# Attention: strided groups laid out residue by residue, rotary sums on GpSimd, exponentials written to PSUM; HGRN gates kept in PSUM

## The reference, cut to what matters

```python
# HGRN2 gates (layer 0)
forget = lb + (1.0 - lb) * sigmoid(f)
key = 1.0 - forget
log_f = log(forget)
query = silu(q)

# dilated attention (layer 1): 12 heads in 3 groups of 4; DILATED_GROUPS = ((128, 1), (512, 4), (2048, 16))
q = apply_rope(qkv[:, :, 0], cos, sin)          # x1*cos - x2*sin, x2*cos + x1*sin
k = apply_rope(qkv[:, :, 1], cos, sin)
# per group: tokens are taken by residue class mod dilation; banded, causal window on each
scores = where(mask, q @ k.T * 128 ** -0.5, -inf)
m = max(scores); p = exp(scores - m); l = sum(p)
out = (p @ v) / l;  lse = m + log(l)
# the three groups' outputs are weighed by softmax(lse) over the groups
o = (stack(outs) * softmax(lse)).reshape(B, S, ATTN_WIDTH) @ w_out
```

## Time and profile before

| | |
|---|---|
| median of 3 runs | 2152.67 us (2152.38 to 2156.83) |
| profiled execution | 2158.04 us |
| its span | 2156.2 us |
| PE busy | 2120.2 us (98%) |
| DVE busy | 995.1 us (46%) |
| ACT busy | 868.8 us (40%) |
| POOL busy | 1149.7 us (53%) |

### The profile page before, as it was taken

How to read it: one execution, slowest core, us unless ns; L and a number is a source line. 1 busy time by engine, 2 the same in 40 slices (tenths; PEclk the granted TensorE clock), 3 DMA queues, 4 the chain that set the end, 5 groups by cost and what they waited for, 6 DMA issues and landing times. The chain is left out here.

```text
span 2156.2 us, 28081 instructions
## 1 busy us (share of the span) xinstructions
PE 2120.2 (98%) x10271; PEld 1750.4 (81%) x10271; DVE 995.1 (46%) x1562; ACT 868.8 (40%) x1250; POOL 1149.7 (53%) x642
## 2 busy tenths in 40 slices
PE   7999999999999999999999999999999999999998
PEld 6788878888888988888888888888667888888886
DVE  6666564403442057745422436563783344422433
ACT  7677653312233234434322334453764234322323
POOL 5677755545554465455554565473224555554552
PEclk9999999999999999999999999999999999999999
DMA  6122133322332322133332332322102223332332
GB/s 214 59 68 68 59 97 94 107 93 88 97 108 80 96 88 69 57 105 98 97 106 89 98 106 89 120 72 89 69 21 79 97 89 98 97 108 85 94 112 70
DMA packets 54423, 195.65 MB, mean 91 GB/s; under 512 B 6832, under 2 KB 9664, under 8 KB 53952
## 3 DMA queue, kind: packets, MB, share of 16 engines
q1 hardware_dynamic: 52864, 187.27, 27.7%
q10 hardware_dynamic: 1472, 7.19, 0.9%
HBM read 190.25 MB, written 4.19 MB: 90 GB/s over the span
## 5 line engine op out<-in xcount | busy, mean ns | idle before, releaser
L1764 POOL TENSOR_TENSOR w_split<-ring,w_split 128x1024 fp32r<-128x1024 f32 (+3 forms) x327 | 841.3, 2573 | 827.1 <-ACT w_split L1237 827.0
L1237 ACT CAST w_split<-ring 128x1024 fp32r<-128x1024 f32 (+3 forms) x327 | 356.4, 1090 | 1007.6 <-PE ps L498 876.1
L496 PE MATMUL ps<-u_split,w_split 128*128 128x512 f32 x1768 | 705.5, 399 | 10.5 <-DVE u_split L2019 9.8
L498 PE MATMUL ps<-u_split,w_split 128*128 128x512 f32 x1768 | 691.0, 391 | 0.0
L497 PE MATMUL ps<-u_split,w_split 128*128 128x512 f32 x1768 | 690.8, 391 | 0.0
L496 PEld LDWEIGHTS ps<-u_split,w_split 128*128 128x128 f32 x1768 | 333.6, 189 | 87.6 <-issue 16.9
L498 PEld LDWEIGHTS ps<-u_split,w_split 128*128 128x128 f32 x1768 | 333.2, 188 | 70.5
L497 PEld LDWEIGHTS ps<-u_split,w_split 128*128 128x128 f32 x1768 | 333.8, 189 | 69.6 <-issue 3.1
L496 PE MATMUL ps<-hid,w_split 128*128 128x512 f32 x637 | 249.0, 391 | 1.5 <-POOL hid L1959 1.4
L498 PE MATMUL ps<-hid,w_split 128*128 128x512 f32 x637 | 247.9, 389 | 0.0
L497 PE MATMUL ps<-hid,w_split 128*128 128x512 f32 x637 | 247.9, 389 | 0.0
(11 more groups left out here) (355 smaller groups left out, 2511.1 us busy)
## 6 DMA issues: line engine op xcount, KB each, us to landing
ring<-in_w_hgrn SPq DMA_DIRECT2D x32, 512.0 KB, 3.6
ring<-in_w_attn_qk SPq DMA_DIRECT2D x24, 512.0 KB, 3.5
ring<-in_w_merge SPq DMA_DIRECT2D x24, 512.0 KB, 3.3
ring<-in_w_gu0a SPq DMA_DIRECT2D x22, 512.0 KB, 3.6
ring<-in_w_gu0b SPq DMA_DIRECT2D x22, 512.0 KB, 3.5
ring<-in_w_gu1a SPq DMA_DIRECT2D x22, 512.0 KB, 3.6
ring<-in_w_gu1b SPq DMA_DIRECT2D x22, 512.0 KB, 3.5
ring<-in_w_gu2a SPq DMA_DIRECT2D x22, 512.0 KB, 3.5
```

Source lines behind the costliest of these rows:

```text
L496: nc.tensor.matmul(ps[:, bank], ws[:, 0, r, w], act[:, 0, c], start=c == 0, stop=False)
L498: m = nc.tensor.matmul(ps[:, bank], ws[:, 1, r, w], act[:, 0, c], start=False, stop=c == n - 1)
L1237: nc.scalar.copy(ws[:, 0, slot, 0:w], ring[:, r, 0:w]).then_inc(s["w_hi"], 1)
L1764: nc.gpsimd.tensor_tensor(ws[:, 1, slot, 0:w], ring[:, r, 0:w], ws[:, 0, slot, 0:w].bitcast(F32), ALU.subtract).then_inc(s["w_lo"], 1)
```

## The change

- `forget` is written back into the PSUM bank of the sigmoid instead of `fg`; `key` is made from there, and the logarithm works in place in that bank, after `key`. The new branches ask `isinstance(head, int)`. `hgrn_forget` and `hgrn_log` are called with a number for heads 0 and 1 alone, ahead of the loop over heads; the calls for heads 2 to 7 stand in the loop and pass pairs, so these keep the old path.
- All query and key tiles except the key tile of group 0 (N % 6 == 1) are written by residue, so that the score matmuls of groups 1 and 2 read 128 neighbouring columns.
- The sum of the rotary step goes from DVE to POOL, behind the cosine product of the same tile. DVE's sine products wait for the sum of tile N-2, as they overwrite its input.
- The exponentials are written to the score banks in PSUM instead of over the masked scores in SBUF; L2419 and L2425 read them there.
- In ACT's list the cast of tile N+5 goes ahead of the wait for the group maxima (`mix_diff`); in the last round so does the cast of `attn_out` unit 3.

```diff
@@ -807,11 +807,10 @@
                         pe.wait_ge(s["ao_lo"], 3 * (j - 1) + (3, 1, 2)[g])
                     q, k = QK[j % 2][:, 2 * g], QK[j % 2][:, 2 * g + 1]
                     for b in range(TT):
+                        qb = q[:, b * P:(b + 1) * P]
                         if g:
-                            m = nc.tensor.matmul(SC_BANKS[g][:, b], q[:, tokens(g, b)], k[:, tokens(g, b)],
-                                                 start=True, stop=True)
+                            m = nc.tensor.matmul(SC_BANKS[g][:, b], qb, k[:, b * P:(b + 1) * P], start=True, stop=True)
                             continue
-                        qb = q[:, b * P:(b + 1) * P]
                         if b:
                             m = nc.tensor.matmul(SC_BANKS[0][:, b], qb, k[:, (b - 1) * P:(b + 1) * P], start=True, stop=True)
                         else:
@@ -1416,6 +1415,10 @@
                 nc.scalar.activation(dst, src, ACT.Sigmoid).then_inc(s[done], 1)
 
             def hgrn_log(head, dst):
+                if isinstance(head, int):
+                    act.wait_ge(s["key"], cnt(head, 1, 1))
+                    nc.scalar.activation(dst, dst, ACT.Ln).then_inc(s["log_f"], 1)
+                    return
                 act.wait_ge(s["forget"], cnt(head, 1, 1))
                 nc.scalar.activation(dst, fg, ACT.Ln).then_inc(s["log_f"], 1)
 
@@ -1518,7 +1521,7 @@
                 act.wait_ge(s["sc_negmax"], 3 * j + score_order(j).index(g) + 1)
                 for b in range(TT):
                     neg, total = (own0[:, k, b:b + 1] if g == 0 else stats[:, k, g, b:b + 1] for k in range(2))
-                    nc.scalar.activation(SC[g][:, b], SC[g][:, b], ACT.Exp, bias=neg, accum_out=total
+                    nc.scalar.activation(SC_BANKS[g][:, b], SC[g][:, b], ACT.Exp, bias=neg, accum_out=total
                                          ).then_inc(s["p_exp"], 1)
 
             for n in range(6):
@@ -1531,20 +1534,21 @@
                 if more:
                     exps(j, 0)
                     exps(j, 1)
+                    qk_weights(N + 5)
                 else:
                     exps(j, 1)
                     hi("attn_out", 2)
                     exps(j, 0)
                     exps(j, 2)
+                    hi("attn_out", 3)
                 act.wait_ge(s["mix_diff"], j + 1)
                 nc.scalar.activation(e_mix, e_mix, ACT.Exp).then_inc(s["mix_exp"], 1)
                 if more:
-                    qk_weights(N + 5)
                     exps(j, 2)
                     take_raw(N + 3, weights=False)
                     take_raw(N + 4)
                 else:
-                    for k in range(3, 6):
+                    for k in range(4, 6):
                         hi("attn_out", k)
                 for n, g in enumerate((1, 2, 0)):
                     act.wait_ge(s["pt_ps"], 3 * j + n + 1)
@@ -1883,8 +1887,19 @@
                     pool.wait_ge(s["rope_scaled"], 2)
                 nc.gpsimd.tensor_tensor(raw[:, N % 2], raw[:, N % 2], cos_a[:], ALU.mult).then_inc(s["rope_cos"], 1)
 
+            def rotary_sum(N):
+                if N >= 12:
+                    pool.wait_ge(s["sc_ps"], 3 * (N // 6 - 1))
+                pool.wait_ge(s["rope_sin"], 2 * N + 2)
+                pool.wait_ge(s["rope_cos"], N + 1)
+                qk, x, y = QK[N // 6 % 2][:, N % 6], raw[:, N % 2], tsin[:, N % 2]
+                if N % 6 != 1:
+                    qk, x, y = by_query(N % 6 // 2, qk), in_order(x), in_order(y)
+                nc.gpsimd.tensor_tensor(qk, x, y, ALU.add).then_inc(s["qk_ready"], 1)
+
             for n in range(24):
                 times_cos(n)
+                rotary_sum(n)
             for k in range(2, 6):
                 lo("attn_out", k)
 
@@ -2269,9 +2284,10 @@
                 x = (head if isinstance(head, int) else head[1]) % 2
                 col = bass.ds(head[0] * 2 + head[1], 1) if not isinstance(head, int) else slice(head, head + 1)
                 dve.wait_ge(s["sig_f"], cnt(head, 1, 1))
-                nc.vector.tensor_scalar(fg, gate, omlb[:, col], lb[:, col], ALU.mult, ALU.add).then_inc(s["forget"], 1)
+                forget = gate if isinstance(head, int) else fg
+                nc.vector.tensor_scalar(forget, gate, omlb[:, col], lb[:, col], ALU.mult, ALU.add).then_inc(s["forget"], 1)
                 dve.wait_ge(s["forget"], cnt(head, 1, 1))
-                nc.vector.tensor_scalar(key[x], fg, -1.0, 1.0, ALU.mult, ALU.add).then_inc(s["key"], 1)
+                nc.vector.tensor_scalar(key[x], forget, -1.0, 1.0, ALU.mult, ALU.add).then_inc(s["key"], 1)
 
             def hgrn_query(head, gate):
 
@@ -2366,16 +2382,12 @@
 
             def rope(N):
                 dve.wait_ge(s["raw_ready"], N + 1)
+                if N >= 2:
+                    dve.wait_ge(s["qk_ready"], N - 1)
                 for lower in (0, 64):
                     src, dst = slice(lower, lower + 64), slice(64 - lower, 128 - lower)
                     nc.vector.tensor_tensor(tsin[dst, N % 2], ps[src, qk_bank(N)], sin_a[src], ALU.mult
                                             ).then_inc(s["rope_sin"], 1)
-                dve.wait_ge(s["rope_sin"], 2 * N + 2)
-                dve.wait_ge(s["rope_cos"], N + 1)
-                qk, x, y = QK[N // 6 % 2][:, N % 6], raw[:, N % 2], tsin[:, N % 2]
-                if N % 6 == 0:
-                    qk, x, y = by_query(0, qk), in_order(x), in_order(y)
-                nc.vector.tensor_tensor(qk, x, y, ALU.add).then_inc(s["qk_ready"], 1)
 
             def masked_max(j, g):
                 n = score_order(j).index(g)
@@ -2416,13 +2428,13 @@
                 dve.wait_ge(s["mix_steps"], 4 * j + 4)
                 both = scm[:, 1024:2048].rearrange("p (b n) -> p b n", b=2 * TT)
                 w12 = e_mix[:, 1:3].rearrange("p g b -> p (g b)")[:, :, None]
-                nc.vector.tensor_tensor(both, both, w12.broadcast_to((P, 2 * TT, P)), ALU.mult).then_inc(s["p_norm"], 1)
+                nc.vector.tensor_tensor(both, ps[:, 6:8].rearrange("p a (b n) -> p (a b) n", b=TT), w12.broadcast_to((P, 2 * TT, P)), ALU.mult).then_inc(s["p_norm"], 1)
                 for r in range(RESIDUES):
                     for b in range(TT):
                         m = nc.vector.tensor_copy(w0[32 * r:32 * r + 32, b:b + 1], e_mix[32 * b:32 * b + 32, 0, r:r + 1])
                 m.then_inc(s["swapped_back"], 1)
                 dve.wait_ge(s["swapped_back"], j + 1)
-                nc.vector.tensor_tensor(SC[0], SC[0], w0[:, :, None].broadcast_to((P, TT, 2 * P)), ALU.mult
+                nc.vector.tensor_tensor(SC[0], SC_BANKS[0], w0[:, :, None].broadcast_to((P, TT, 2 * P)), ALU.mult
                                         ).then_inc(s["p_norm"], 1)
 
             def ao_rest(j):
```

## The result

| | before | after |
|---|---|---|
| median | 2151.86 us (19 runs, 2148.43 to 2156.83) | 2155.21 us (19 runs, 2153.57 to 2157.14) |
| profiled execution | 2158.04 us | 2154.19 us |
| its span | 2156.2 us | 2152.4 us |

The ratio is 1.0019, with a 95% interval from 1.0013 to 1.0024. So the changed kernel is 3 to 5 us slower, where 9.9 us of gain were forecast, and its median lies 4 us above the range. The two profiled executions compare the other way round (2154.19 against 2158.04). That contrast is the first half of the answer: the profiled execution of before was not like most of its executions.

A forecast was written before the change was run, and what follows sets the result against it. PE, busy 2120.2 of 2156.2 us, was taken as the bound. -7.1 (HGRN) -7.0 (scores) +4.2 (waits) = -9.9 us took the profiled 2158.04 to 2148.1; with the median 5.4 lower, 2142.8, range 2136 to 2151.

The forecast's parts named there:

- The 5.2 us: PE's single wait on the HGRN score gather (L2186), traced to head 1's key product taking 9.11 us on DVE beside POOL.
- change 1: HGRN gates of heads 0 and 1 in PSUM: removes 5.15 us of wait and 1.9 of half clock, together 7.1.
- Rival E: HGRN: PE finds another late releaser at 53 us, gain 0 of 7.1, 2149.9 us; chance 0.08.
- Change 2: Attention score matmuls of groups 1 and 2 read contiguous columns: 1.76 us saved a round, 7.0 in four rounds.
- Change 3: Rotary sums moved from DVE to POOL: 1.4 us each, so POOL's cycle of 5.1 fits PE's tile of 5.44.
- Rivals C and D: Rotary sum on POOL takes about 2.1 us: 2149.8, chance 0.09; or 2.6, pacing all 24 tiles: 2162, chance 0.06.
- The round worked out: Attention round 0 scheduled by hand: PE waits 0.6 for group 0's probabilities and 1.1 for cast 12; all rounds +4.2 us.
- rival B: Attention: POOL also blocks the 16 mix copies, chain ends some 2.6 us later, 7.8 in three rounds, 2150.6; chance 0.15.
- The cast itself: Cast 11 moved ahead in ACT's list: pays for itself, avoiding 1.6 us a round, with no gain beyond the matmul saving.
- rival A: POOL doesn't get in DVE's way at L2401 and L2414 in attention: 5.6 us less, 2137.2; chance 0.20.
- Waits behind the core: PE waits after attention's core for the next cast: 1.1 us in round 0; tile 23's sum 0.5 late in round 3.
- Change 4: Attention exponentials written to PSUM: under 0.1 us a round, counted as nothing; effect is 0.9 and the blocking within the round.

The follow-up runs named there:

- one-element experiment: The changed kernel with each of the 16 two-element copies of the mix split into two one-element copies: 2147.03 us, ratio 0.9983 to before.
- layout alone: The kernel before with only tiles written by residue and contiguous score matmuls of groups 1 and 2, sums still on DVE: 2154.97 us, ratio 1.0019.
- second profile of before: The kernel before, nothing edited, profiled once more: 2152.72 us, span 2150.9.
- copies as reductions: The changed kernel with the 16 two-element copies of the mix done as maxima over one element: 2146.31 us, ratio 0.9964 to before.
- exponentials back in SBUF: The changed kernel with exponentials written over the masked scores in SBUF and read there by the two products: 2158.11 us, ratio 1.0039 to before.
- attention alone: The changed kernel without its HGRN lines, so HGRN as before: 2159.58 us, ratio 1.0028 to before.
- moved cast back: The changed kernel with the cast of tile N+5 back behind the mix exponential in ACT's list: 2150.84 us, ratio 0.9999 to before.
- the version that beats both: copies as reductions, plus POOL's low part of the first unit behind the core put ahead of the sum: 2143.89 us, ratio 0.9968 to before.
- HGRN alone: The kernel before with only the diff's HGRN lines (heads 0 and 1 through PSUM): 2150.3 us, ratio 0.9985.
- sums back on DVE: The changed kernel with the rotary sums back on DVE, still written by residue: 2154.54 us, ratio 1.0004 to before.

## Why the prediction was wrong, point by point

**What bounds it: right.** PE's program, its waits and the clock behind them are the only places where the time changed.

**The 5.2 us, and change 1: the mechanism right, its weight in the median wrong.** `key` from PSUM takes 0.69, the scans follow at 48.1, no wait and no low clock are left near 60. The term of -7.1 was real in the profiled execution and is absent from most. The clue was on the table: the profiled execution took 5.4 us more than the median, and the wait was 5.15. I carried those 5.4 us over as a constant to both kernels, where they were the wait itself. Where the wait is there, 7.1 was the right size (6.7 us between the two profiles of before). The right term for a median is about 1 us. Rival E's price was thus nearly right, but by luck, as its mechanism was not: no other releaser took over, and PE reached that point on time.

**Change 2: right.** 64 matmuls from 15.7 to 7.9 us of duration, and 1.7 us a round in the distance of starts.

**Change 3, the price of the sum: right.** Its 24 instances took (ns, min/median/max) what the contiguous cosine product takes, although 20 of them write by residue:

```profile
L1898 POOL TENSOR_TENSOR arena<-arena x24: 1273/1302/1317, 741.0 to 903.9; 128x512 f32<-128x512 f32 x24
```

I had 1.4. No tile paces on POOL. Rivals C and D fell.

**The round worked out: one line of it failed.** "16 copies (2.75) to 798.4" took over a row that had been measured with POOL idle, into a schedule where POOL is busy; it measured 5.95. The prediction named this as rival B, with POOL's work at the right moment, and gave it 0.15, because the copies of L2422 had run beside POOL unharmed. Those have one element a partition and these have two; the one-element experiment shows that this was no evidence. B said 2.6 us a round later; the wait on the last product is 2.59 against the forecast 0.6, so 2.0 more, in three rounds, and 1.37 in the last. B had the copies wait as a whole for the cast to end; in the trace they begin, and single ones among them wait (the longest 2.31 us). Of rival B, the Trainium skill (SBUF — State Buffer, section "Who interferes with whom") states that copies in a two-port mode contend with GpSimd and that `tensor_reduce` never does on trn2, and that issue order decides who is blocked. The runs here agree on the first two: 5.95 us for the copies, 2.58 for the reductions. The third the prediction left out, as it spoke of DVE alone as blocked. For it the trace of before has one pair of rows: L2419 of round 0 began at 804.42 and took its usual 1.22 us, and POOL's cast, begun at 804.80, took 3.09 for 2.40. The 9.11 us of one `key`, over the ends of seven instructions of POOL, are more than a single blocked turn. The same skill (VectorE: DVE Perf Modes, section "Mode 2×_2P — use both read ports for one tensor") has that mode read the two halves of one tensor through two ports. As I read it, a single element leaves nothing to halve; the one-element copies (131 to 152 ns, none held off) agree.

**The cast itself: wrong in sign.** It "pays for itself", I wrote. In the changed kernel it costs about 4 us (4.4 by the medians, 3.2 in waits), since it is what the copies wait for longest. With moves that POOL can't hold off it harms only the one product behind them (1.2 us); the reductions with the cast put back were not run.

**The product behind the copies (against rival A): right.** L2413 took 0.17 us in after, which looks like A, but only since the copies ended behind the cast. With the copies out of the way it was held off as forecast (1.40 us). And L2426, the later product of two SBUF tensors, took 1.16 us in after itself, until POOL's cosine product ended at 797.89. A is refuted.

**Waits behind the core: right in rounds 0 and 1.** 0.78 and 0.82 us at tiles 12 and 18, for 1.1 worked out. The 0.5 us of round 2 and the 0.5 for tile 23's sum did not come in after.

**Change 4: no term of its own, about right in the round.** The prediction counted 0.9 us less for L2425 and no blocking of L2419. Taken back, it costs 2.9 us by five executions: 0.6 in waits and 1.7 in clock by the profile. The layout alone shows what L2419 can cost from SBUF, 2.82 to 3.38 us.

**The clock: not in the sum.** 1.7 us, behind a wait of 2.60 us in round 2. I had counted the clock that the change would give back in HGRN, and none that its new waits would take.

With B in place of the forecast round and no gain in HGRN, the sum of the prediction reads -7.0 + 4.2 + 7.8 = +5.0 us. Measured is +2.8 to +5.2, but that this fits is partly luck: B's 7.8 stands for 5.2 us of waits beyond the forecast 5.6 and for the 1.7 of clock, which B didn't have, and 1 us of HGRN is left out. The measured terms are -7.0 in matmuls, +9.4 in waits, +1.7 in clock and -1.0 ahead of attention, +3.1 us.

## What to carry to other kernels

A duration belongs to what ran beside it: before a row of DVE is carried into a new schedule, look at what POOL did during it, and whether the instruction is of a form that POOL held off here (a copy or `tensor_scalar` from SBUF to SBUF with two or more elements a partition, or a product of two SBUF sources). A reduction, a one-element copy or a source in PSUM took it out of the contest. Where the profiled execution lies as far above the median as one of its waits is long, that wait may be absent from the median, and its removal worth next to nothing there; a second profile of the same kernel shows it. Two spans of single executions are compared safely only where both went through the same clock changes. Taking time out of PE's program pays only as far as the chain that feeds its next wait gets shorter too.

## What the runs showed of the hardware that I had not expected

- Starvation over many instructions: one `key` product waited 9.11 us behind a row of POOL's products and casts, although there is a boundary between any two of them; in another execution it got in at the first one (0.65 us). Which of the two happens differs between executions of one kernel, and its share between groups of runs: 9 of 31, 1 of 19, none of 22, none of 14. What decides it is open.
- A write by residue costs POOL nothing (1.27 to 1.32 us for 128x512, contiguous or not), and DVE a good deal: 1.10 to 1.12 us against 0.69.
- In most executions PE's clock also falls once in the third layer, which the change doesn't touch. Windows of the second profile of before:

```profile
1496.00:1500.00 4.00, 4.00 (x47) 4.00 (x45) 0.00 (x0) 0.00 (x0) 0.00 (x0) 0.65 0.02 4
1500.00:1504.00 4.00, 4.00 (x18) 3.49 (x17) 3.41 (x4) 0.00 (x0) 0.00 (x0) 0.50 0.00 0
```

In copies as reductions the same stretch has 1.00 throughout. The cost can be read from PE's own starts: from the last matmul of L1012 (L1011 and L1140 in the kernels built on the changed one) to the first of L1141, a stretch that is the same program in all twelve profiled executions.

| last start to first start | profiled executions |
|---|---|
| 38.9 to 39.0 us | copies as reductions, exponentials back in SBUF |
| 41.6 to 41.7 us | before, after, attention alone, layout alone, moved cast back, one-element copies, the version that beats both |
| 43.2 to 43.3 us | before's second profile, HGRN alone, sums back on DVE |

So it costs nothing, 2.6 or 4.3 us. This fits the spread of 5 us within one heap: of the 58 executions of before in the lower heap, in the three groups of runs beside the experiments, the 12 fastest (2147.8 to 2148.9 us) have a mean granted clock of 0.998 or 0.999 over the whole run, and the other 46 (2149.9 to 2153.3) have 0.996 or 0.997. PE is busy with small matmuls when the clock falls, and nothing in the traces tells what decides it.
